# Delta scan with three state buffers, attention per 64-query chunk, and a projection's 24 narrow columns with 512 tokens moving

## The reference

```
v_new = u - w @ state
o     = q_dec @ state + qk @ v_new
state = dec * state + k_upd^T @ v_new
```

## Time and profile before

| | us |
|---|---|
| median of 3 runs | 1611.95 (1609.96 to 1613.9) |
| the profiled execution, its own time | 1608.53 |
| span of its trace | 1606.7 |
| busy: PE / DVE / ACT / POOL | 1367.2 / 1115.8 / 708.4 / 308.9 |
| share of the span: PE / DVE / ACT / POOL | 85% / 69% / 44% / 19% |

### The profile page before, as it was taken

The page is one execution under the profiler, slowest core; times in us unless marked ns, Lnnn a source line. Parts: engine busy times, 40 slices in busy tenths (PEclk is TensorE's granted clock), DMA queues, the critical chain, the costliest instruction groups (busy, mean ns, idle before and its releaser), DMA issues. The chain is left out here.

```text
span 1606.7 us, 15933 instructions
## 1 busy us (share of the span) xinstructions
PE 1367.2 (85%) x6216; PEld 1052.5 (66%) x6216; DVE 1115.8 (69%) x1283; ACT 708.4 (44%) x877; POOL 308.9 (19%) x130
## 2 busy tenths in 40 slices
PE   4899976759776996999999958957899689999993
PEld 1587765549765455788888744425764678888882
DVE  3757665667554364999999945865306659999995
ACT  1212333132123231877777823124622257778771
POOL 2100000000000000255545410000000015554541
PEclk9879997879888986999999978977879689999997
DMA  9688327220300334999999654460001669999964
GB/s 346 225 270 288 107 79 263 65 79 14 118 1 1 118 142 179 342 389 373 376 380 379 244 197 170 152 251 38 1 0 40 234 221 370 381 382 384 383 251 182
DMA packets 63329, 337.92 MB, mean 210 GB/s; under 512 B 11754, under 2 KB 11834, under 8 KB 49172
## 3 DMA queue, kind: packets, MB, share of 16 engines
q1 hardware_dynamic: 50868, 310.54, 51.9%
q0 software_dynamic: 11568, 22.91, 4.0%
q10 hardware_dynamic: 816, 3.43, 0.6%
HBM read 325.82 MB, written 28.84 MB: 221 GB/s over the span
## 5 line engine op out<-in xcount | busy, mean ns | idle before, releaser
L1388 PE MATMUL ps<-ring_r,work_r 128*128 128x512 f32 x536 | 211.9, 395 | 0.0
L2378 DVE TENSOR_TENSOR ring_r<-ring,early_mod_r 128x2048 fp32r<-128x2048 f32 x76 | 188.7, 2513 | 25.2 <-ACT early_mod_r L1543 24.7
L1543 ACT ACTIVATE work<-ps 128x512 f32<-128x512 f32 (+4 forms) x139 | 87.8, 637 | 242.3 <-PE ps L1388 135.7
L1386 PE MATMUL ps<-early_mod_r,work_r 128*128 128x512 f32 x468 | 187.8, 401 | 7.7 <-DVE work_r L2684 4.7
L823 POOL TENSOR_TENSOR work<-work,early_mod 128x1024 f32<-128x1024 f32 x30 | 156.3, 5208 | 159.4 <-ACT work L1543 159.4
L926 PE MATMUL ps<-const,work 128*128 128x128 f32 x792 | 125.6, 302 | 67.5 <-ACT work L1543 13.2
L1387 PE MATMUL ps<-early_mod_r,work_r 128*128 128x512 f32 x468 | 182.9, 391 | 0.0
L926 PEld LDWEIGHTS ps<-const,work 128*128 128x128 f32 x792 | 105.7, 159 | 90.4 <-issue 15.4
L1543 ACT ACTIVATE work_r<-ring 128x2048 fp32r<-128x2048 f32 (+2 forms) x87 | 133.3, 1556 | 55.5 <-PE ps L935 55.5
L1543 ACT ACTIVATE early_mod_r<-ring 128x2048 fp32r<-128x2048 f32 x79 | 147.6, 1909 | 0.4 <-PE ps L1388 0.3
L1386 PE MATMUL ps<-work_r 128*128 128x512 f32 x324 | 132.3, 408 | 6.8 <-DVE work_r L2684 4.7
(11 more groups left out here) (335 smaller groups left out, 2738.2 us busy)
## 6 DMA issues: line engine op xcount, KB each, us to landing
ring<-in_moe_w_up_dram SPq DMA_DIRECT2D x33, 2048.0 KB, 10.3
early_mod<-in_ada_w_dram SPq DMA_DIRECT2D x80, 512.0 KB, 4.7
ring<-in_moe_w_gate_dram SPq DMA_DIRECT2D x19, 2048.0 KB, 9.5
hT<-in_moe_w_down_dram SPq DMA_DIRECT2D x16, 2048.0 KB, 9.6
ring<-in_moe_w_down_dram SPq DMA_DIRECT2D x15, 2048.0 KB, 9.9
work<-in_moe_w_gate_dram SPq DMA_DIRECT2D x14, 2048.0 KB, 10.3
ring<-in_ab_w_in_dram SPq DMA_DIRECT2D x7, 2048.0 KB, 9.6
ring<-in_ada_w_dram SPq DMA_DIRECT2D x4, 2048.0 KB, 23.9
```

What stands on the lines that cost most here:

```text
L1386: mm(out, a_lo, w_hi, start=first_, stop=False)
L1388: return mm(out, a_hi, w_lo, start=False, stop=last_)
L1543: return nc.scalar.activation(out, in_, fn, **kw)
L2378: v.tensor_tensor(half_of(l, m, half, True), half_of(l, m, half), highs[(2 * m + half) % MHIGHS].bitcast(F32), ALU.subtract).then_inc(SV.s ...
```

## The change

- **Narrow chunk.** The 24 columns become the stationary side and all 512 tokens move: 24 matmuls into 24 rows of bank 0, one copy by DVE into a new `smallT` (24 rows of 512, a 25th row of ones), and at n = 2 four transposes, of which the eight GDN columns are copied to `psm`. The first matmuls of n = 2 wait for that one copy.
- **GLA gates.** z is made from `smallT` and a second operand padded with zero rows (one parameter load in place of two). The four transposes, the copy and the clearing of `gaT` go.
- **Delta scan.** Three state buffers, used in turn; the output products leave the recurrence and stand behind `gdn_solve(t + 1)`, in banks 0 and 5 by turns. Decay rows of t+1 come after the first w @ state, key products after the first update, transposes after the second w @ state. The head norm of tile t-1 lies within tile t. `rep` and the copy of u go from DVE to ACT. Part of `mod_sums` moves into the last tile. The preparation of tile 0 starts with the transposes and the solve; its `rep` is made before the inverses.
- **Between the layers.** The modulation columns come before the first combine, the normed columns of tile 0 before the combine of tile 2.
- **Attention.** Each chunk of 64 queries is multiplied by exactly the 128 keys that it sees: 16 products of 256 moving columns per tile, with 64 stationary columns. Maximum and exponentials read PSUM directly, per key/value head; the division comes before the transposes (16 per tile); the value products have the values stationary (64 columns) and write the output already transposed. Seven copies of 64 KB within SBUF, on SP's queue ahead of the second experts' loads, bring the values of each two chunks together. The mask constant (196 KB of a load), the clearing L2519, L2505, L2535 and the output's transposes go.
- **Overflow.** An outer If around the loops for a second and further overflow blocks, on PE, ACT, DVE and POOL.

The diff, cut to its core and with twelve columns of indentation removed:

```diff
-            for t in range(TT):
+            for t in ((0, ) if kind == "small" else range(TT)):
                 j = 4 * n + t
                 if q == 0 and n:
                     pe.wait_ge(*emptier(j - 4))
+                if q == 0 and n == 2 and t:
+                    pe.wait_ge(*emptier(j - 8))
                 for k in range(2):
                     kk = 2 * q + k
                     first_, last_ = kk == 0, kk == KD - 1
                     if kind[0] == "f":
                         ins = parts_mm(bank(t), (high[:, k, cols(t)], low[:, k, cols(t)]), (hT_high[:, kk], hT_low[:, kk]), first_, last_)
+                    elif kind == "small":
+                        ins = parts_mm(bank(t)[0:SMALL], (high[:, k], low[:, k]), (hT_high[:, kk], hT_low[:, kk]), first_, last_)
                     else:
-                        w = 24 if kind == "small" else 512
-                        ins = parts_mm(bank(t)[:, 0:w], (hT_high[:, kk, cols(t)], hT_low[:, kk, cols(t)]), (high[:, k], low[:, k]), first_, last_)
+                        ins = parts_mm(bank(t), (hT_high[:, kk, cols(t)], hT_low[:, kk, cols(t)]), (high[:, k], low[:, k]), first_, last_)
                 if q == 3:
-                    ins.then_inc(proj_pe.sem, proj_pe.one("job"))
+                    ins.then_inc(proj_pe.sem, sum(proj_pe.one("job") for _ in range(TT if kind == "small" else 1)))
+            if n == 2 and q == 1:
+                pe.wait_ge(*emptier(4))
+                for t in range(TT):
+                    ins_ = turn(bank(6, TT, 32)[:, t, 0:SMALL], smallT[0:SMALL, cols(t)], SMALL)
+                ins_.then_inc(GATE_PE.sem, GATE_PE.one("small"))
...
     for t in range(TT):
-        ins = turn(bank(0)[0:RANK, cols(t)], psm[:, t, 0:RANK])
-    ins.then_inc(GATE_PE.sem, GATE_PE.one("gaT"))
-    pe.wait_ge(GATE_DVE.sem, GATE_DVE.at(0, "gaT"))
-    for t in range(TT):
         o = 256 * (t % 2)
-        ins = mm(bank(2 + t // 2)[:, o:o + 256], gaT[0:RANK + 1, cols(t)], w2aug[0:RANK + 1, :], start=True, stop=True)
+        ins = mm(bank(2 + t // 2)[:, o:o + 256], smallT[0:SMALL + 1, cols(t)], w2aug[0:SMALL + 1, :], start=True, stop=True)
...
+    for hd in range(HEADS):
+        mm(o[:, cols(hd)], qkt[:, b, hd], vn[:, hd], start=(hd == 0), stop=False, skip_group_check=True)
+    for c in range(2):
+        r = slice(CHUNK * c, CHUNK * c + CHUNK)
+        for hd in range(HEADS):
+            ins = mm(o[r, cols(hd)], qd_b[:, b, hd, r], st_b[:, (2 * t + c) % 3, hd], start=False, stop=True, skip_group_check=True)
+    ins.then_inc(GDN_PE.sem, GDN_PE.one("o"))
...
 def gdn(t):
-    b = t % 2
-    if t + 1 < TT:
-        gdn_prep(t + 1)
-    if t:
-        turn_output_b(t - 1)
+    b, ahead = t % 2, t + 1 < TT
     pe.wait_ge(GDP_ACT.sem, GDP_ACT.at(t, "wT"))
-    if t:
-        pe.wait_ge(GDN_DVE.sem, GDN_DVE.at(t - 1, "on"))
-        pe.wait_ge(GDN_ACT.sem, GDN_ACT.at(t - 1, "ss"))
     for c in range(2):
         r = slice(CHUNK * c, CHUNK * c + CHUNK)
         if c:
             pe.wait_ge(GDN_DVE.sem, GDN_DVE.at(t, "s0"))
+        elif t:
+            pe.wait_ge(GDN_DVE.sem, GDN_DVE.at(t - 1, "s1"))
         for hd in range(HEADS):
-            ins = mm(bank(4)[r, cols(hd)], wt_b[:, b, hd, r], st_b[:, hd], start=True, stop=True)
+            ins = mm(bank(4)[r, cols(hd)], wt_b[:, b, hd, r], st_b[:, (2 * t + c) % 3, hd], start=True, stop=True)
         ins.then_inc(GDN_PE.sem, GDN_PE.one(f"ws{c}"))
+        if c == 0 and ahead:
+            gdn_rows(t + 1)
+        if c == 1 and ahead:
+            gdn_kv(t + 1)
+        if not ahead:
+            if c == 0:
+                pe.wait_ge(GDP_DVE.sem, GDP_DVE.at(t, "ku"))
+                pe.wait_ge(GDP_ACT.sem, GDP_ACT.at(t, "u"))
+                pe.wait_ge(sums_in[0], 16)
+            mod_sums(0, 2 * c, 2 * c + 2)
+        if c == 1 and t:
+            turn_output_b(t - 1)
         pe.wait_ge(GDN_DVE.sem, GDN_DVE.at(t, f"vn{c}"))
+        if c == 0:
+            pe.wait_ge(GDP_DVE.sem, GDP_DVE.at(t, "ku"))
         for hd in range(HEADS):
-            mm(bank(0)[r, cols(hd)], qd_b[:, b, hd, r], st_b[:, hd], start=True, stop=False)
-            ins = mm(bank(0)[r, cols(hd)], qkt[:, b, hd, r], vn[:, hd], start=False, stop=True)
-        ins.then_inc(GDN_PE.sem, GDN_PE.one(f"o{c}"))
-        for hd in range(HEADS):
-            ins = mm(bank(5)[:, cols(hd)], ku_b[:, b, c, hd], vn[:, hd], start=True, stop=True)
+            ins = mm(bank(4)[:, cols(hd)], ku_b[:, b, c, hd], vn[:, hd], start=True, stop=True)
         ins.then_inc(GDN_PE.sem, GDN_PE.one(f"up{c}"))
-    if t + 1 < TT:
+        if c == 0 and ahead:
+            gdn_kq(t + 1)
+    if ahead:
         gdn_solve(t + 1)
+    gdn_out(t)
...
+    for g in range(NKV):
+        if t:
+            pe.wait_ge(SCO_ACT.sem, SCO_ACT.at(t - 1, f"exp{g}"))
+        for n in (2 * g, 2 * g + 1):
+            for c in range(2):
+                r = slice(CHUNK * c, CHUNK * c + CHUNK)
+                at_ = P * t + CHUNK * c
+                ins = mm(bank(g)[r, 256 * (n % 2):256 * (n % 2) + 256], qT[:, n, at_:at_ + CHUNK],
+                         kTz[:, g, :, at_:at_ + 2 * CHUNK], start=True, stop=True)
...
+    for c in range(2):
+        v_ = pkv[:, t, 256 * c + HD * g:256 * c + HD * g + HD]
+        for par_ in range(2):
+            o = bank(6 + g % 2)[HD * par_:HD * par_ + HD, 0:256].rearrange("p (n q) -> p n q", n=2)[:, :, CHUNK * c:CHUNK * c + CHUNK]
+            ins = mm(o, v_, pg[:, par_, :, CHUNK * c:CHUNK * c + CHUNK], start=True, stop=True)
...
     scores(0)
     for t in range(TT):
         if t + 1 < TT:
             scores(t + 1)
-        values(t)
-        if t == TT - 1:
-            pe.wait_ge(SCO_DVE.sem, SCO_DVE.at(t, "s7"))
-            pe.wait_ge(sums_in[2], 16)
-            mod_sums(1, 0, 4)
-        turn_output(t)
+        pe.wait_ge(v_moved, 16 * (2 * t + 1))
+        turn_weights(t, 0)
+        for g in range(NKV):
+            if g + 1 < NKV:
+                turn_weights(t, g + 1)
+            values(t, g)
+            if t == TT - 1 and g == 1:
+                pe.wait_ge(SCO_ACT.sem, SCO_ACT.at(t, "exp3"))
+                pe.wait_ge(sums_in[2], 16)
+                mod_sums(1, 0, 4)
     mod_sums(1, 4, 8)
...
         over_block(0)
-        with pe.Fori(1, MAXOVER) as j:
-            with pe.If(n_over > j):
-                over_turn(j)
-                over_block(j)
+        with pe.If(n_over > 1):
+            with pe.Fori(1, MAXOVER) as j:
+                with pe.If(n_over > j):
+                    over_turn(j)
+                    over_block(j)
...
-                    if emptied[j][0] == "v":
+                    if emptied[j][0] == "v" and not (kind == "small" and t):
                         dve.wait_ge(proj_pe.sem, proj_pe.at(j, "job"))
                         src = bank(t)
                         dst = {"qk": pqk[:, t], "v": pv[:, t]}.get(kind)
                         if kind == "small":
-                            dst, src = psm[:, t], src[:, 0:24]
+                            dst, src = smallT[0:SMALL, :], src[0:SMALL]
                         elif kind[0] == "f":
                             dst = qkvT[:, j - 12, 3:3 + SEQ]
                         v.tensor_copy(dst, src).then_inc(proj_dve.sem, proj_dve.one("ev"))
+            if n == 2 and q == 3:
+                dve.wait_ge(GATE_PE.sem, GATE_PE.at(0, "small"))
+                v.tensor_copy(psm[:, :, RANK:SMALL], bank(6, TT, 32)[:, :, RANK:SMALL]).then_inc(GATE_DVE.sem, GATE_DVE.one("small"))
...
 def gdn(t):
     S, b, ahead = GDN_DVE, t % 2, t + 1 < TT
-    dve.wait_ge(GDP_DVE.sem, GDP_DVE.at(t, "u"))
+    dve.wait_ge(GDP_ACT.sem, GDP_ACT.at(t, "u"))
     for c in range(2):
         r = slice(CHUNK * c, CHUNK * c + CHUNK)
+        k = 2 * t + c
         dve.wait_ge(GDN_PE.sem, GDN_PE.at(t, f"ws{c}"))
         v.tensor_tensor(vn[r], u_b[r, b], bank(4, HEADS, P)[r], ALU.subtract).then_inc(S.sem, S.one(f"vn{c}"))
-        if ahead:
-            if c == 0:
-                gdn_prep_decays(t + 1)
-            else:
-                gdn_prep_solve(t + 1)
+        if c == 0 and t:
+            head_variance(t - 1)
+        if c == 1 and ahead:
+            gdn_prep_solve(t + 1)
+            gdn_prep_decays(t + 1)
         dve.wait_ge(GDN_PE.sem, GDN_PE.at(t, f"up{c}"))
         for hd in range(HEADS):
-            ins = v.scalar_tensor_tensor(out=st_b[:, hd], in0=st_b[:, hd], scalar=pexp[:, 3 + c, t, hd:hd + 1],
-                                         in1=bank(5)[:, cols(hd)], op0=ALU.mult, op1=ALU.add)
+            ins = v.scalar_tensor_tensor(out=st_b[:, (k + 1) % 3, hd], in0=st_b[:, k % 3, hd], scalar=pexp[:, 3 + c, t, hd:hd + 1],
+                                         in1=bank(4)[:, cols(hd)], op0=ALU.mult, op1=ALU.add)
         ins.then_inc(S.sem, S.one(f"s{c}"))
+        if c == 0 and t:
+            head_norm(t - 1)
         dve.wait_ge(S.sem, S.at(t, f"s{c}"))
-        if ahead and c == 0:
-            gdn_prep_products(t + 1)
     if ahead:
```

(27 more changed lines are left out.)

420 lines of the change are left out of this document (214 added, 206 removed).

## The result

| | before | changed |
|---|---|---|
| median, us | 1610.95 (1607.51 to 1613.9, 4 runs) | 1505.3 (1503.53 to 1508.47, 4 runs) |
| ratio, 95% interval | | 0.9347 (0.9322 to 0.9372) |
| span of the profiled execution | 1606.7 | 1503.9 |
| busy PE / DVE / ACT | 1367.2 / 1115.8 / 708.4 | 1285.6 / 1100.1 / 698.0 |

A forecast was written before the change was run, and what follows sets the result against it. PE and loads bound the expert phases, dependency chains the delta scan and attention. Narrow chunk -3, scan -45, between the layers -6 and attention -41 sum to -95, from 1611.95 to 1517 us; range 1498 to 1542.

The forecast's parts named there:

- base case: Whole kernel: all terms hold as counted, 95 us less, 1517 us, spanning 1508 to 1532; chance 0.60.
- rival C: Attention: score and value products writing different halves of the output rows overlap, 14 us less, 1503 us; chance 0.14.
- Preparation of tile 0: Delta scan: from the inverses' end to w @ state 8.3 us in place of 22.6, start at 427.3, -14.3 us.
- The order of its steps: Scan tile: solve, outputs, w @ state, v_new, update, state, last tile's norm, second v_new, in a 13.6 us period.
- PE's 12.4 us per tile: Attention: PE work per tile, scores 7.0, transposes 1.8 and values 3.6 us, where it was 16.8.
- they follow at once on DVE and ACT, about 1 us: Between the layers: tile 0's normed columns directly follow its transposes, first job of the second projection at 966.9, -6.3 us.
- The step on the chunk itself: First projection: PE waits for DVE's copy behind a late-loaded side accumulation, so the next chunk starts at 100.4, -2.7 us.
- The step after it: From narrow chunk to total: the chunk's gain of 3 us was counted in full in the sum of -95.
- z's 4 us: GLA gates: z could start 4 us earlier, but the gate waits for side loads arriving at 278.8, so 0.
- rival A: Narrow chunk: not held up because the load lands early, the full -13 us, 1507 us; chance 0.05.
- B: Scan and attention: chains longer than counted, tiles of 18 us each, 28 us more, 1545 us; chance 0.15.
- D: Scan and attention: granted clock falls to 1.2 GHz through both new stages, adding 115 us, 1632 us; chance 0.02.

## Why the prediction was right, and where it was off

The time lies inside the range, but below the base case's own 1508 to 1532 and nearest to rival C. The range held because it reached down to C. Between the two spans the kernel gained 102.8 us against 95: the attention gave 13 more and the scan 3 more than forecast, the narrow chunk and the stretch between the layers 2 less each, and the expert phases took some 5 back. That these partly cancel is luck.

**Scan, -45 forecast, -48.3 measured.** Preparation of tile 0: -14.3 forecast, -14.5 measured; w @ state starts at 426.25, forecast 427.3. Tiles: period 13.6 forecast, 12.91 measured. The order of its steps held: the norm stands between the new state and the second v_new. What the sum missed is that the last outputs and the next tile's first product overlap: from the end of the second v_new to the next w @ state it takes 5.2 us, where the forecast had 5.9. PE's work, forecast at 12.1 us, is 12.4 of the 12.9, so PE now holds the tile as much as the chain does. Last tile: 16.9, forecast 17.

**Attention, -41 forecast, -54.0 measured** (0.6 of it in the second projection). The mis-sized term is PE's 12.4 us per tile: scores were costed at 16 x 0.44 = 7.0 and take 3.7, of the 3.3 us of difference 2.6 by running side by side (6.3 against 3.7) and 0.7 because a call costs less than the proportion to 128 columns said; the four groups of value products take about 0.6 us each to the next instruction, 2.4 instead of 3.6. The period is 10.5 us, where rival C said 10.7 and the base case 14.3, and C's 1503 is 2.3 us from the measured 1505.3. With the scores half by half the kernel took 1514.4, within the base case. Its chance of 0.14 was too low: the rows of before could not show it, since no two neighbouring calls there wrote to different halves, and silence of the rows was counted as evidence against it. The Trainium skill, "TensorEngine Tiling (Array Packing)", section Key Properties, says that different tiles work in parallel: these runs agree, with 3.7 against 6.3 us at the full clock.

**Between the layers, -6 forecast, -4.3 measured:** the step "they follow at once on DVE and ACT, about 1 us" took 0.7 us more than that, and 1.2 us were lost ahead of the transposes, which the forecast kept where they were. Why the first combine's load came later was not settled; the 19.6 to 21.7 us over the other versions show that this stretch moves by 2 us.

**Narrow chunk, -3 forecast, about -1 measured.** The step on the chunk itself was right to 0.6 us. The projection up to its last matmul gained 3.7 us by the run with the chunk undone, as forecast. The step after it failed, and the prediction had the reason in hand: it let z's 4 us vanish in the wait for the late side loads, and passed the chunk's 3 us through the same wait. Two 2 MB chunks stand ahead of those loads in SP's queue. Nor would an earlier chunk 2 have brought more, as rival A's 13 us had it: in the run with the moved copy it started 6.2 us earlier and the projection ended at the same time.

**Rivals.** A: refuted, the load came at 99.0. B: no, tiles are shorter, not longer. D: the granted clock was 1.00 through the whole scan and 0.94 in the attention, where the waits became short. By the forecast's own mark, that it is wrong "if the attention ends under 60" us after its start, the base case failed in that stage (56.3). Two further terms were not foreseen: the first experts took 2.7 us more (0.8%, under the forecast's mark of 1%), and the last stretch 2.3 more, which lies within what two executions of one program differ by. The overflow block shows a part, on PE's timeline of the changed kernel:

```profile
887.96 0.63 PE L1416 MATMUL ps<-work_r 128*128 128x512 f32 x1
888.39 0.63 PE L1417 MATMUL ps<-ring_r,work_r 128*128 128x512 f32 x1
...
892.65 0.49 PE L1415 MATMUL ps<-work_r 128*128 128x512 f32 x1
892.98 0.40 PE L1416 MATMUL ps<-work_r 128*128 128x512 f32 x1
```

Its first 12 matmuls take 0.43 us from start to start, the later ones 0.23: the low level of 1.2 GHz and then 2.4. Before, the same block ran at 0.23 throughout. That is 2.4 us, in products that the change did not touch. Over the profiles the number of slow matmuls differs: 12 and 13 in the two of the changed kernel, 6 to 14 in nine other versions with the outer If, but none in the one with the norm ahead, which has it too, and none in the two kernels without it. So the outer If goes together with the low clock here, but it does not decide it alone, and what does was not settled.

## What to carry to other kernels

Products with 64 output rows took 0.6 of the time when neighbours wrote to different halves (3.7 against 6.3 us for 16 of 256 columns), so give the two chunks of a tile to the two halves and keep calls of both next to each other. Behind a wait for a transfer, an earlier stage's gain disappears: follow each saved microsecond to the next wait for a load before it is counted, and put work that depends on late loads where its engine would stand idle, not ahead of a product that others wait for. In a recurrence, take off the chain all that only reads the state, and put it where it covers another engine's copy.

## What was not expected of the hardware

Calls to different halves overlap even across instructions of different kinds and across a wait that has been met: the outputs of one tile and the first product of the next (0.05 us from start to start). An order of two and two did as well as strict alternation (3.77 and 3.75 us). And a kernel whose edit showed nothing up to the experts was 4 us shorter inside them in its profile, with the same code there: differences under 5 us between versions of this program were trusted only where the stage that was edited showed them.
